# Transformer block on one core: the spacer products of TensorE in five seams become fp32r products with broken-up columns

## The reference

```python
def squared_relu_mlp(h, w_up, w_down):
    u = jax.nn.relu(h @ w_up)
    return (u * u) @ w_down

for layer in range(DEPTH):                     # DEPTH = 2
    if layer < N_A:                            # layer 0: gated recurrence
        mix = hgrn2_mixer(rms_norm(h, a_norm_pre[a]), a_w_in[a], lb_all[a], a_gate_norm[a], a_w_out[a])
        h = h + rms_norm(mix, a_norm_post[a])
    else:                                      # layer 1: differential attention
        mix = diff_attn_mixer(rms_norm(h, b_norm_pre[bi]), k_sh, v_sh, b_w_q[bi], ...)
        h = h + rms_norm(mix, b_norm_post[bi])
    ff = squared_relu_mlp(rms_norm(h, mlp_norm_pre[layer]), mlp_w_up[layer], mlp_w_down[layer])
    h = h + rms_norm(ff, mlp_norm_post[layer])
    if layer == N_A - 1:
        k_sh, v_sh = shared_kv(h, kv_norm, w_kv)
...
h = rmsnorm(x, mix_pre_norm[i])                # second block
z = h @ w_in[i]
a = mla(...)
c = short_gated_conv(...)
x = x + rmsnorm(m @ w_out[i], mix_post_norm[i])
f = (jax.nn.silu(h @ w_gate[i]) * (h @ w_up[i])) @ w_down[i]
x = x + rmsnorm(f, ffn_post_norm[i])
x = x + jax.nn.sigmoid(x @ w_ple_gate[i]) * e
```

## Time and profile before

| | |
|---|---|
| time of three runs, us | 965.34 (median), 964.89 to 965.67 |
| span of the profiled execution, us | 963.2 |
| PE busy | 952.3 us, 99% of the span |
| DVE / ACT / POOL busy | 78% / 57% / 9% |
| granted TensorE clock, mean | 0.999 of full speed |

### The profile page before, as it was taken

One profiled execution on the slowest core, in us unless ns is written; L12 is line 12 of the kernel. 1 busy time (PEld: TensorE's weight loads), 2 busy tenths in 40 slices (PEclk: granted clock), 3 DMA queues, 4 the chain that ended last, 5 costly groups with the idle time before them and its releaser, 6 DMA issues.

```text
span 963.2 us, 18430 instructions
## 1 busy us (share of the span) xinstructions
PE 952.3 (99%) x7530; PEld 909.1 (94%) x7530; DVE 748.2 (78%) x1129; ACT 547.7 (57%) x819; POOL 89.4 (9%) x91
## 2 busy tenths in 40 slices
PE   9999999999999999999999999999999999999998
PEld 8999999999999998999999999999999999999998
DVE  6998778978855599867987844489887998787777
ACT  6652366656454476756665544455666665556455
POOL 5334101000201000001000201001001000000000
PEclk9999999999999999999999999999999999999999
DMA  8733444766666836436476575626636467665651
GB/s 256 243 120 115 143 128 140 218 200 197 195 183 193 267 109 197 150 113 183 136 215 197 176 214 184 194 68 182 183 110 202 127 197 214 187 190 170 203 175 44
DMA packets 164723, 166.62 MB, mean 173 GB/s; under 512 B 6784, under 2 KB 162832, under 8 KB 164640
## 3 DMA queue, kind: packets, MB, share of 16 engines
q1 hardware_dynamic: 162752, 163.47, 55.5%
q0 software_dynamic: 1056, 1.19, 0.5%
q10 hardware_dynamic: 832, 0.79, 0.4%
HBM read 163.82 MB, written 1.08 MB: 171 GB/s over the span
## 4 chain that ended last, share of the span: by engine, by line
PE 82%; DVE 12%; issue 2%; ACT 2%; DMA 2%; SPq 0%; POOL 0%; ACTq 0%; DVEq 0%
PE ps L657 19%; PE ps L660 16%; PE ps L649 13%; DVE w_lo L1990 4%; PE ps L676 3%; PE ps L677 3%; PE ps L678 3%; PE ps L682 2%; PE ps L683 2%; PE ps L684 2%; PE ps L689 2%; PE ps L609 2%; PE ps L617 2%; PE ps L690 2%; PE ps L691 2%
## 5 line engine op out<-in xcount | busy, mean ns | idle before, releaser
L1990 DVE TENSOR_TENSOR w_lo<-w_raw,w_hi 128x1024 fp32r<-128x1024 f32 (+4 forms) x314 | 375.0, 1205 | 116.1 <-ACT w_hi L1424 110.3
L1424 ACT ACTIVATE w_hi<-w_raw 128x1024 fp32r<-128x1024 f32 x298 | 313.3, 1056 | 200.3 <-PE ps L660 47.6
L657 PE MATMUL ps<-xs,w_hi 128*128 128x256 f32 x1012 | 132.6, 277 | 0.0
L657 PEld LDWEIGHTS ps<-xs,w_hi 128*128 128x128 f32 x1012 | 127.0, 188 | 4.5
L660 PE MATMUL ps<-xs,w_lo 128*128 128x256 f32 x832 | 112.2, 277 | 0.0
L660 PEld LDWEIGHTS ps<-xs,w_lo 128*128 128x128 f32 x832 | 102.9, 188 | 0.2
L682 PE MATMUL ps<-xs,w_hi 128*128 128x256 f32 x320 | 91.4, 285 | 0.4 <-DVE w_lo L1990 0.4
L683 PE MATMUL ps<-xs,w_hi 128*128 128x256 f32 x320 | 89.3, 279 | 0.0
L684 PE MATMUL ps<-xs,w_lo 128*128 128x256 f32 x320 | 89.3, 279 | 0.0
L649 PE MATMUL ps<-xs,w_hi 128*128 128x512 f32 x326 | 85.1, 393 | 0.3 <-DVE mo L2018 0.2
L1431 ACT ACTIVATE tmp<-ps 128x512 f32<-128x512 f32 x75 | 44.5, 593 | 70.6 <-PE ps L649 62.6
(11 more groups left out here) (431 smaller groups left out, 1896.6 us busy)
## 6 DMA issues: line engine op xcount, KB each, us to landing
w_raw<-in_mlp_w_up SPq DMA_DIRECT2D x64, 512.0 KB, 4.2
w_raw<-in_mlp_w_down SPq DMA_DIRECT2D x64, 512.0 KB, 3.5
w_raw<-in_a_w_in SPq DMA_DIRECT2D x32, 512.0 KB, 4.3
w_raw<-in_w_gate SPq DMA_DIRECT2D x22, 512.0 KB, 3.8
w_raw<-in_w_up SPq DMA_DIRECT2D x22, 512.0 KB, 4.6
w_raw<-in_w_down SPq DMA_DIRECT2D x20, 512.0 KB, 4.4
w_raw<-in_w_kv SPq DMA_DIRECT2D x16, 512.0 KB, 4.3
w_raw<-in_w_in SPq DMA_DIRECT2D x16, 512.0 KB, 3.9
```

The lines of the kernel that those rows point to most:

```text
L657: mm(ps[:, 2 * pset + n, at], hi[:, kk, n * P:(n + 1) * P], x[:, kt0 + kk, at], start=False, stop=False)
L1424: o = fn(dst, raw, ACT.Copy)
L1990: return v.tensor_tensor(d, x, y, ALU.subtract)
```

## The change

A new helper `stream_shapes` takes the place of `keep_streaming` in five seams: all of the six-product calls (`ak0`, `up1`, `cq`, `pg`) and the call of four in `up0`. The single spacer ahead of `bucket_rows` and the two of seam `gu` stay as they were. The helper first waits for `lo_ready` of both quanta of the next matrix's first unit, then reads that unit's `w_hi` slots: slot `s0` gives the stationary operand, seven 128-column pieces in turn, slot `s1` the moving one. It issues seven products for each shape in its list. A shape is (n, run, same):

- n is the number of columns, S = 256 or 2S = 512.
- run > 0: the moving columns come in turn from the first and the second half of the n columns, in pieces of `run` columns. run = -2 or -4: every second or every fourth column, then the next set.
- same: the result is written to the bank in that same broken-up order (True) or to neighbouring columns (False).

```diff
+            def stream_shapes(name, shapes, bank=B6):
+
+                s0, s1 = slot_of(UNIT0[name], 0), slot_of(UNIT0[name], 1)
+                pe.wait_ge(lo_ready, 2 * UNIT0[name] + 2)
+
+                def order(row, n, run):
+                    if run == 0:
+                        return row[:, 0:n]
+                    if run < 0:
+                        return row[:, 0:n].rearrange("p (i r) -> p r i", r=-run)
+                    if run == 1:
+                        return row[:, 0:n].rearrange("p (a i) -> p i a", a=2)
+                    return row[:, 0:n].rearrange("p (a i r) -> p i a r", a=2, r=run)
+
+                for n, run, same in shapes:
+                    x = order(w_hi[:, s1, :], n, run)
+                    o = order(ps[:, bank, :], n, run if same else 0)
...
+                    for j in range(7):
+                        mm(o, w_hi[:, s0, P * j:P * j + P], x, start=True, stop=True)
...
-            keep_streaming(4, B7)
+            stream_shapes("up0", ((S, 1, False), (S, 2, False), (S, 4, False), (S, 16, False)), B7)
...
-            keep_streaming(6)
+            stream_shapes("ak0", ((S, 2, True), (S, 4, True), (S, 16, True), (S, -2, False)))
...
-            keep_streaming(6)
+            stream_shapes("up1", ((2 * S, 2, False), (2 * S, 4, False)))
...
-            keep_streaming(6)
+            stream_shapes("cq", ((2 * S, 2, True), (2 * S, 1, False)))
...
-            keep_streaming(6)
+            stream_shapes("pg", ((2 * S, 8, True), (S, 8, True), (S, -4, False)))
```

More of the change, by code:

```diff
@@ L826, in keep_streaming @@
                     mm(ps[:, bank, 0:S], ident, table[:, T_IDENT:T_IDENT + S], start=True, stop=True)
+            def stream_shapes(name, shapes, bank=B6):
[12 more added lines that the diff above has]
+                    o = order(ps[:, bank, :], n, run if same else 0)
+                    if run > 1 and not same:
+                        o = o.rearrange("p (i a r) -> p i a r", a=2, r=run)
+                    elif run == 1 and not same:
+                        o = o.rearrange("p (i a) -> p i a", a=2)
+                    elif run < 0 and not same:
+                        o = o.rearrange("p (r i) -> p r i", r=-run)
+                    for j in range(7):
+                        mm(o, w_hi[:, s0, P * j:P * j + P], x, start=True, stop=True)
             pe.wait_ge(blank_ready, 1)
```

## The result

| | before | after |
|---|---|---|
| median of 5 runs each, us | 965.34 | 969.21 |
| lowest to highest, us | 964.89 to 966.60 | 968.91 to 970.00 |
| span of the profiled execution, us | 963.2 | 967.1 |

The ratio is 1.0037, with an interval of 1.0024 to 1.0051: slower by 3.9 us (2.3 to 4.9) where 3.6 was forecast. The total was right, in part by luck: two of the steps behind it were false, and most of what follows is about that.

What follows compares the result with a forecast made beforehand. PE was taken to bound the kernel, busy 952.3 of 963.2 us. Terms `up0` 2.0, `cq` 1.0, `pg` 0.55, `ak0` and `up1` 0, together +3.6 on 965.34, gave 968.9 us; range 966.4 to 973.2.

Steps and rivals of the forecast that it cites:

- What bounds the kernel: Whole kernel: PE, busy 952.3 of 963.2 us at full clock; added PE work costs its time unless PE was waiting anyway.
- Columns at full speed, +1.3: Five seams, broken-up order left aside: the new streams cost +1.3 us, all in `up0`, where the stream outlasts its room.
- `up0` +2.0: Seam `up0`: 1.3 us for plain columns plus 7 x 0.10 for its products in pieces of 1, 2.0 us.
- Pieces of 1 run at the float32 pace: Single-column products in `up0` and `cq`: 0.216 instead of 0.113 us, +0.10 per 256 columns, +0.20 per 512.
- rival of full speed: All seams: columns run at full speed whatever their order, only `up0` pays, +1.3 us, 966.6 us; chance 0.30.
- Pieces of 2 jump no more often than L917, so nothing: Products in pieces of 2 and more, all seams: they jump no more often than float32 L917 did, costed at nothing.
- rival of slow pairs: All seams: broken reads with jumps at up to pieces of 2 run at half rate, +7.6 us, 972.9 us; chance 0.12.
- Every second and fourth column at the float32 pace: Seven products each in `ak0` and `pg`: float32 pace, adding 0.72 us in `ak0` and 0.7 in `pg`.
- `ak0` gives its lateness back at DVE's wait: Seam `ak0`: of 0.72 us added, 0.25 is room, the rest lies in PE's 0.48 wait for DVE at 361.96; cost 0.
- `up1` 0: Seam `up1`: the stream ends at 456.56 with 0.23 us of room left, so it costs 0.
- `cq` 1.0: Seam `cq`: 7 x 0.20 for pieces of 1 plus 0.14 late, 1.55, less the 0.54 wait for POOL behind: 1.0 us.
- `pg` 0.55: Seam `pg`: 0.7 us for seven products of every fourth column, less 0.16 of room: 0.55 us.

## Why the prediction was right in its sum and wrong in its terms

- **What bounds the kernel**: right. PE's work costs what doesn't fit into a wait, seam by seam, and the clock stayed full.
- **Columns at full speed, +1.3**: right. With neighbours +1.4, and the whole of it in `up0` (with pieces of 1 +1.45, and half the products there give 0.1).
- **`up0` +2.0**: +1.83 in the trace and +2.0 alone. Right in size by luck, for a wrong reason: see the next two.
- **"Pieces of 1 run at the float32 pace"**: this step failed. They take 112 and 216 ns, less than neighbours. L917, in float32 and with every second column of one run after another, said nothing on two runs in turn. The rival of full speed had this right, and its test (a start every 0.113 us) was met.
- **"Pieces of 2 jump no more often than L917, so nothing"**: failed too. They take 166 and 328 ns. L917 takes a column in 0.90 ns, the fp32r product at this pace one in 0.65: a price that shows at fp32r pace is covered at float32's. The rival of slow pairs had the kind right and the size wrong: 1.5 times, not 2, and not every second column of the sum. All pieces of 2 give +6.95.
- **Every second and fourth column at the float32 pace**: right, 230 and 233 ns where 216 was reckoned. But in `ak0` that meets the pieces of 2: the stream takes 4.67 us instead of 3.9, and behind the first tile PE is 3.15 late (345.67 against 342.52) where the stream began 1.85 late.
- **"`ak0` gives its lateness back at DVE's wait"**: right, and more than was counted. The printed idle time of 0.48 runs from the modelled end of the record before; from start to start PE stood for 361.96 - 361.21 = 0.75, of which a product back to back needs 0.12: 0.63 to give. In the kernel after the same records follow at 364.35 and 364.47, and the lateness falls from 3.14 to 2.51. A further wait of 0.32 for DVE ahead of L1038 at 368.37, which the prediction didn't look up, takes 0.2. Left: 0.25 instead of 0, which isn't more than two traces differ by.
- **`up1` 0**: failed with the pieces of 2. The stream takes 4.24 instead of 3.20, and no wait follows: 0.65 left.
- **`cq` 1.0**: wrong on both sides. Pieces of 2 of 512 columns cost 7 x 0.10 and those of 1 nothing, where 1.4 was put, so 3.99 us instead of 4.6. Behind it POOL's wait gave 0.70, not 0.54, by the same reckoning (652.55 - 651.73 - 0.12). No idle time is printed there now. 0.55 less lateness is left at `pg`, without a wait that was found for it, and the seam leaves -0.29; the others, with nothing to give back, have -0.13 to 0.45 in this stretch.
- **`pg` 0.55**: the traces leave 1.44, of which about 0.85 is the stream's. Pieces of 8 at 124 and 244 ns and the filling (0.2 behind the float32 sums) take the room; the stream takes 4.37 instead of 3.9. And after the entry PE loses 0.37 more: the twelve products of a tile take 1.36 us in the kernel before (937.89 to 939.25) and 1.42 in that after (940.05 to 941.47), 0.113 and 0.118 each. The kernels with only `up0` changed, with neighbours and with pieces of 1 have the 0.118 too and lose 0.3 to 0.5 behind the entry, so this isn't the broken-up columns: it is the one trace of the kernel before that is quicker here, and why wasn't found.
- **Writes in pieces at nothing**: right, for pieces of 2 and more.
- **The wait for `lo_ready` at nothing**: right, no row shows PE waiting there.

By the two traces the forecast was 1.3 too high in `cq`, 0.25, 0.65 and 0.9 too low in `ak0`, `up1` and `pg`, and right in `up0` by two errors that cancel: together 0.3 off. Of these `cq` and `up1` stand; that of `ak0` is within what one trace differs from another, and 0.6 of that of `pg` too. That the sum came out is luck, and the total alone would have confirmed a rule that is the wrong way round.

## What to carry to other kernels

Price a reading pattern from rows at the pace at which it will be read: a slower format hides what a faster one pays. Where an fp32r product has its moving operand in one row, let it read single columns of two halves in turn if the operand can be stored so by an engine that walks half by half; here that was worth 1.4%. And check a forecast term by term, since a sum within 0.3 us of the measurement stood on two steps that were both false; and take more than one trace before a term of half a microsecond is believed.

## What the runs showed that was not expected

- An fp32r product reads single columns of two runs in turn in 112 ns per 256 and 216 per 512; neighbours take 113 to 120 and 226 to 231. The first are 0.44 and 0.42 ns per column, near one per cycle of 2.4 GHz. Why neighbours lose some per cent was not shown.
- A step of 2 in the moving columns doubles an fp32r product's time (226 to 230 ns), a step of 4 is no worse (233), pieces of 4 and more are nearly free (128 to 120), and pieces of 2 from two runs take 166.
- Writing by turns into two halves costs ACT 1156 ns instead of 633 and DVE 1195 instead of 754 on 512 columns; reading at every second column 801 and 831.
- Taking the spacers away lowers the granted clock of the stages behind to between 0.77 and 0.91 in four places of five, and costs 6.1 us.
